# All low parts of the weights on VectorE while the gates of the experts are made

## The chip, the cores and the metric

One core of a Trainium2 chip runs the kernel. The metric is the device time of one execution in microseconds (us). The kernel before was run three times: the median is 3381.05 us, the runs lie between 3377.15 and 3381.17 us. All arithmetic is float32 in effect: TensorE is fed each operand as a high and a low part.

## The reference

The reference is a small network on 256 tokens of width 1024. Ahead of everything else stands a block of two layers, each an attention-like mixer followed by a product-key expert layer (`peer`). After it comes a second block of two layers (feed-forward, four kinds of attention, feed-forward). The change touches the two expert layers alone. Cut to what matters:

```
def peer(x, w_q, subkeys, u_tab, v_tab):
    q = (xf @ w_q).reshape(N, PEER_HEADS, 2, PEER_QHALF)
    s = jnp.einsum('nhpd,hpkd->nhpk', q, subkeys)
    ...
    idx = jnp.take_along_axis(cand_i, best_pos, axis=-1)
    g = jax.nn.softmax(best_s, axis=-1)
    ...
    act = jax.nn.gelu(jnp.einsum('nd,nhkd->nhk', xt, u_tab[it]), approximate=False)
    return jnp.einsum('nhk,nhkd->nd', gt * act, v_tab[it])
```

Each token picks 8 x 16 of 16384 experts. The kernel computes the products with all 16384 rows of `u_tab`, and multiplies the result by a gate matrix that is zero for the experts which a token did not pick; then it multiplies by all of `v_tab`.

## The kernel before, in words

**Weights.** All weights come as 933 units of 128 x 1024 values (512 KB each), which SyncE loads into a ring of four slots (`RAW`, line 2566). A unit is two halves of 128 x 512; the kernel has 1866 halves, numbered `j`. For each half ScalarE copies the raw weight to a rounded high part `WH` (line 1031, `Scalar.split`), and then VectorE or GpSimd subtracts it from the raw weight, which gives the low part `WL` (line 1587, `Vector.split`, or line 2321, `Gpsimd.split`). Here "a low" is one such subtraction. TensorE waits for the low part (line 422, `Tensor.half`) and multiplies three times: high by high, high by low, low by high (line 404). `WH` and `WL` are rings of five halves, so that ScalarE makes the high part of half `j` only when TensorE is through with half `j - 5` (line 1030). A slot of `RAW` is loaded again when the low parts of both of its halves are there (lines 2564 and 2565).

**Who makes a low.** The function `low_on_pool` (line 32) decides it from `j` alone. Its answer is used in four places: in `Vector.split`, in `Gpsimd.split`, and in `Chip.lo`, by which TensorE and SyncE choose the semaphore they wait for. As a rule every fourth half goes to GpSimd (`j % 4 == 3`); in a stretch of 256 halves in each expert layer, every second one does (line 37).

**The expert layer.** `peer_stage` of each engine writes out the order of work: 32 halves for the queries, 256 halves of `u_tab` (groups 0 to 127 of 128 experts), 256 halves of `v_tab`. The gates of groups 0 to 63 (part 0) are made beside the products with groups 64 to 127 of `u_tab`; the gates of groups 64 to 127 (part 1) are made beside the products with groups 0 to 63 of `v_tab`. The stretch of line 37 is just these 256 halves: it begins five halves later than TensorE's count, since the splits run five halves ahead.

**A step of the gates.** A part has 64 steps, one per four tokens, and each engine's `gates` generator is advanced at a rate of 0.55 steps per half (`Pace.tick`). In step s VectorE makes two one-hot tiles, OHA (line 2081, 4 x 128 columns) and OHB (line 2087, 4 x 64 columns). OHB weighted with three parts of the gate gives OHW: ScalarE makes the first part with four instructions (line 1370), GpSimd the second (line 2450), VectorE the third (line 2094). TensorE then runs 12 matmuls of 64 columns (lines 836 to 839), two steps behind, and in every second step VectorE multiplies G, the activations in SBUF, with the result in PSUM (line 2104). OHB of step s waits for all three products of step s - 2 (lines 2084 to 2086); TensorE waits for the same three (lines 832 to 834). GpSimd's product of step s waits for OHB of step s and for the gate matmuls of step s - 2 (lines 2445 to 2447). In VectorE's program a tick's step stands ahead of the tick's low: OHA, OHB, OHW, G in every second step, then lows until the next step. In part 1 there is also GL, the low part of a group of activations (line 2112), once for every two halves.

All two-input operations of VectorE named here read both inputs from SBUF, except G, which reads one from PSUM. Both operations of GpSimd read SBUF.

Of the kernel before, what the change touches and what calls it, by code (L numbers as in the profile page):

```python
# [31 lines left out]
def low_on_pool(j):  # L32

    for layer in range(DEPTH):
        up = BASE[PEER[layer]] + 32 + 2 * GP + NHALF
        if up <= j < up + 4 * (128 - GP):
            return j % 2 == 1
    for end in BASE[1:]:
        if end + 1 <= j <= end + 4:
            return False  # L40
    return j % 4 == 3
# [82 lines left out]
class Chip:  # L124
# [68 lines left out]
    def lo(self, j):  # L193
        return (self.lo_p if low_on_pool(j) else self.lo_v).at(j)
# [1378 lines left out]
class Vector:  # L1573
# [6 lines left out]
    def split(self):  # L1580

        c, e, j = self.c, self.e, self.made
        self.made += 1
        if j < N_HALVES and not low_on_pool(j):
            raw, wh, wl = c.low(j)
            e.wait_ge(*c.hi.at(j))
            e.tensor_tensor(wl, raw, wh.bitcast(F32), ALU.subtract).then_inc(*c.lo_v.mark(j))  # L1587
# [719 lines left out]
class Gpsimd:  # L2307
# [6 lines left out]
    def split(self):  # L2314

        c, e, j = self.c, self.e, self.made
        self.made += 1
        if j < N_HALVES and low_on_pool(j):
            raw, wh, wl = c.low(j)
            e.wait_ge(*c.hi.at(j))  # L2320
            e.tensor_tensor(wl, raw, wh.bitcast(F32), ALU.subtract).then_inc(*c.lo_p.mark(j))  # L2321
# [444 lines left out]
```

## Time and profile before

| | |
|---|---|
| median of 3 runs | 3381.05 us |
| the profiled execution, its own time | 3373.28 us |
| its span in the trace | 3371.3 us |
| TensorE (PE) matmuls busy | 3067.7 us, 91% |
| VectorE (DVE) busy | 2358.2 us, 70% |
| ScalarE (ACT) busy | 1828.7 us, 54% |
| GpSimd (POOL) busy | 1147.1 us, 34% |
| lows on VectorE | 1281, 992.5 us |
| lows on GpSimd | 585, 870.5 us |
| mean granted TensorE clock | 0.975 of full speed |

All times in rows are us from the start of the span unless marked ns. An instruction's duration in the trace runs from its start to its end; instructions of one engine can overlap by a little, so the distance from start to start is what an engine spends on one. A row such as "A <- B: x, n" says that engine and operation A sat idle x us in n cases until B released it. The share of busy time is an average over stages with different limits.

### The profile page before, as it was taken

What the parts mean: (1) busy time and instruction counts of PE and PEld (TensorE: products, weight loads), DVE (VectorE), ACT (ScalarE), POOL (GpSimd) and SP (SyncE); (2) the same over time, 40 slices, a digit from 0 to 9 for tenths busy, and PEclk for the clock granted to TensorE, in tenths of its full rate; (3) what the DMA queues carried; (4) which work ended last, traced back from release to release, by engine and by line L of the source; (5) the groups of instructions that cost most, each with busy time, mean ns of one, the idle gap of its engine ahead of it and who ended that gap; (6) DMA issues with size and microseconds to landing.
All of it is one profiled execution on the core that took longest, in us unless ns stands there. A gap on an engine that the chain in (4) does not pass through costs nothing.

```text
span 3371.3 us, 58728 instructions
## 1 busy us (share of the span) xinstructions
PE 3067.7 (91%) x21820; PEld 2730.0 (81%) x21820; DVE 2358.2 (70%) x4217; ACT 1828.7 (54%) x4063; POOL 1147.1 (34%) x883
## 2 busy tenths in 40 slices
PE   8899988888899889998888889979997999998899
PEld 7699988866688779998886668869876998977798
DVE  4559999899945555999989994564566545456644
ACT  5455566666555445556666555545544555554454
POOL 1113366666522111335666652222110223211121
PEclk9999999999999999999999999989999999999999
DMA  5345543433455325554343335545522555542254
GB/s 208 107 169 169 176 138 132 145 126 125 132 197 196 129 88 169 170 175 138 132 145 126 126 125 202 196 166 191 167 98 82 185 188 193 184 161 82 100 188 157
DMA packets 139532, 512.77 MB, mean 152 GB/s; under 512 B 15713, under 2 KB 16242, under 8 KB 137970
## 3 DMA queue, kind: packets, MB, share of 16 engines
q1 hardware_dynamic: 134352, 489.22, 43.4%
q10 hardware_dynamic: 4898, 19.81, 1.6%
q8 instruction: 175, 2.87, 0.3%
q14 instruction: 107, 0.88, 0.1%
HBM read 507.92 MB, written 1.05 MB: 151 GB/s over the span
## 4 chain that ended last, share of the span: by engine, by line
PE 59%; DVE 25%; issue 8%; POOL 3%; ACT 3%; DMA 1%; DVEq 0%; ACTq 0%; POOLq 0%; SPq 0%
PE ps L404 58%; DVE GAIN L2081 5%; DVE WL L1587 4%; DVE GAIN L2087 4%; DVE OHW L2094 2%; POOL WL L2321 2%; DVE GL L2112 2%; POOL OHW L2450 1%; ACT WH L1031 1%; PE ps L408 1%; ACT BIG L1127 1%; DVE BIG L1699 0%; DVE BIG L1748 0%; DMA RAW<-in_w 0%; DVE XTl L1626 0%
## 5 line engine op out<-in xcount | busy, mean ns | idle before, releaser
L1031 ACT ACTIVATE WH<-RAW 128x512 fp32r<-128x512 f32 x1866 | 1165.4, 628 | 1037.4 <-PE ps L404 1010.8
L2321 POOL TENSOR_TENSOR WL<-RAW,WH 128x512 fp32r<-128x512 f32 x585 | 870.5, 1488 | 2096.6 <-ACT WH L1031 2096.6
L1587 DVE TENSOR_TENSOR WL<-RAW,WH 128x512 fp32r<-128x512 f32 x1281 | 992.5, 779 | 777.7 <-ACT WH L1031 770.7
L404 PE MATMUL ps<-XTh,WH 128*128 128x256 f32 x3928 | 1139.4, 290 | 22.1 <-DVE XTl L1795 8.3
L404 PE MATMUL ps<-XTl,WH 128*128 128x256 f32 x3928 | 1123.1, 286 | 0.0
L404 PE MATMUL ps<-XTh,WL 128*128 128x256 f32 x3928 | 1122.1, 286 | 0.0
L404 PEld LDWEIGHTS ps<-XTh,WH 128*128 128x128 f32 x3928 | 765.5, 195 | 33.4 <-DVE WL L1587 14.1
L404 PEld LDWEIGHTS ps<-XTl,WH 128*128 128x128 f32 x3928 | 766.2, 195 | 3.1
L404 PEld LDWEIGHTS ps<-XTh,WL 128*128 128x128 f32 x3928 | 765.3, 195 | 0.0
L404 PE MATMUL ps<-WH,GH 128*128 128x512 f32 x1408 | 569.9, 405 | 70.4 <-DVE GL L2112 59.6
L404 PE MATMUL ps<-WL,GH 128*128 128x512 f32 x1408 | 553.4, 393 | 0.0
L404 PE MATMUL ps<-WH,GL 128*128 128x512 f32 x1408 | 552.0, 392 | 0.0
L404 PEld LDWEIGHTS ps<-WH,GH 128*128 128x128 f32 x1408 | 266.6, 189 | 137.1 <-DVE GL L2112 68.8
L1370 ACT ACTIVATE OHW<-GAIN,GT 128x64 bf16<-128x64 bf16 x1024 | 270.4, 335 | 107.3 <-DVE GAIN L2087 104.4
L404 PEld LDWEIGHTS ps<-WH,GL 128*128 128x128 f32 x1408 | 266.5, 189 | 57.7
L404 PEld LDWEIGHTS ps<-WL,GH 128*128 128x128 f32 x1408 | 267.2, 190 | 46.7
L2450 POOL TENSOR_TENSOR OHW<-GAIN,GT 128x256 bf16<-128x256 bf16 x256 | 232.2, 908 | 79.9 <-DVE GAIN L2087 79.9
L2081 DVE TENSOR_TENSOR GAIN<-CST,AB 128x512 bf16<-128x512 f32 x256 | 233.0, 910 | 0.0
L404 PEld LDWEIGHTS ps<-OHW,GAIN 128*128 128x128 bf16 x3072 | 106.0, 98 | 143.3 <-issue 125.0
L404 PE MATMUL ps<-OHW,GAIN 128*128 128x64 bf16 x3072 | 133.5, 194 | 89.2 <-DVE OHW L2094 66.8
L2087 DVE TENSOR_TENSOR GAIN<-CST,AB 128x256 bf16<-128x256 f32 x256 | 204.0, 797 | 9.7 <-issue 5.1
L404 PE MATMUL ps<-BIG 128*128 128x64 f32 (+6 forms) x966 | 153.6, 311 | 21.0 <-DVE BIG L1774 4.5
(181 smaller groups left out, 2679.9 us busy)
## 6 DMA issues: line engine op xcount, KB each, us to landing
RAW<-in_w SPq DMA_DIRECT2D x933, 512.0 KB, 3.3
BIG<-in_ln ACTq DMA_DIRECT2D x4, 1024.0 KB, 5.1
GAIN<-in_norms ACTq DMA_DIRECT2D x6, 512.0 KB, 4.2
BIG<-in_sk ACTq DMA_DIRECT2D x2, 1024.0 KB, 4.8
BIG<-in_na_bias ACTq DMA_DIRECT2D x2, 1024.0 KB, 10.5
BIG<-in_qk_gain ACTq DMA_DIRECT2D x2, 960.0 KB, 7.2
BIG<-in_memT ACTq DMA_DIRECT2D x4, 256.0 KB, 7.6
BIG<-in_xT ACTq DMA_DIRECT2D x1, 1024.0 KB, 5.1
```

The lines of the kernel that those rows point to most:

```text
L404: return self.e.matmul(out, lhsT, rhs, start=start, stop=stop, skip_group_check=loose)
L408: return self.e.transpose(out, in_, self.c.IDENT[0:n, 0:n])
L1031: e.activation(wh, raw, ACT.Copy).then_inc(*c.hi.mark(j))
L1127: e.activation(t.E[:, i % 3, w], src[:, w], ACT.Exp, bias=s[:, blk:blk + 1], accum_out=s[:, 2 + blk:3 + blk]).then_inc(*c.exps.mark(tag, i ...
L1370: t = e.activation(c.OHW[:, r, 0, k * GP:k * GP + GP], c.OHB[:, r, k, :], ACT.Copy, scale=c.GT0[:, 4 * s + k:4 * s + k + 1])
L1587: e.tensor_tensor(wl, raw, wh.bitcast(F32), ALU.subtract).then_inc(*c.lo_v.mark(j))
L2081: e.tensor_tensor(c.OHA[:, step % 3], ia, c.AB[:, 0, n4].unsqueeze(2).to_broadcast([P, 4, 128]), ALU.is_equal).then_inc(*c.vec.mark())
L2087: e.tensor_tensor(c.OHB[:, step % 2], ib, c.AB[:, 1, n4].unsqueeze(2).to_broadcast([P, 4, GP]), ALU.is_equal).then_inc(*c.one.mark(stage, ...
L2094: e.tensor_tensor(c.OHW[:, s % 2, 2, :].rearrange("p (k n) -> p k n", k=4), c.OHB[:, s % 2], c.GT[:, 2, 4 * s:4 * s + 4].unsqueeze(2).to_b ...
L2112: e.tensor_tensor(c.GL[:, r, :], c.peer.G[:, g, :], c.GH[:, r, :].bitcast(F32), ALU.subtract).then_inc(*c.xtl.mark(stage, "g", g))
L2321: e.tensor_tensor(wl, raw, wh.bitcast(F32), ALU.subtract).then_inc(*c.lo_p.mark(j))
L2450: e.tensor_tensor(c.OHW[:, r, 1, :].rearrange("p (k n) -> p k n", k=4), c.OHB[:, r], c.GT[:, 1, 4 * s:4 * s + 4].unsqueeze(2).to_broadcast ...
```

## The change

It replaces one line in `low_on_pool`. In the stretch of 256 halves in each expert layer the function now answers False, where it said True for every odd `j`. So 128 lows in each of the two layers move from GpSimd to VectorE, which makes 1537 instead of 1281; GpSimd keeps 329 of 585. Nothing else is changed: neither the order of the work, nor the rate of the gates, nor who makes the three products OHW.

```
--- before.py
+++ after.py
@@ -34,7 +34,7 @@
     for layer in range(DEPTH):
         up = BASE[PEER[layer]] + 32 + 2 * GP + NHALF
         if up <= j < up + 4 * (128 - GP):
-            return j % 2 == 1
+            return False
     for end in BASE[1:]:
         if end + 1 <= j <= end + 4:
             return False
```

## Rows read from the trace of the kernel before

**Rows 1.** The page, part 1: busy time of each engine, share, instructions
```profile
PE 3067.7 (91%) x21820; PEld 2730.0 (81%) x21820; DVE 2358.2 (70%) x4217; ACT 1828.7 (54%) x4063; POOL 1147.1 (34%) x883
```
**Rows 2.** Stretches of the four gate parts: engines' busy us, clock, DMA share, GB/s
```profile
core 0: us, PE busy (x) PEld busy (x) DVE busy (x) ACT busy (x) POOL busy (x), PEclk, DMA share, GB/s
425.50:650.60 225.10, 198.38 (x2123) 191.54 (x2122) 221.07 (x278) 143.47 (x395) 151.34 (x121) 0.99 0.41 136
...
671.70:911.90 240.20, 196.76 (x1440) 148.42 (x1441) 235.66 (x335) 146.48 (x424) 155.97 (x121) 0.99 0.38 127
...
1520.40:1746.10 225.70, 201.81 (x2129) 195.04 (x2128) 218.65 (x278) 143.74 (x396) 150.96 (x121) 0.98 0.40 134
...
1767.20:2009.60 242.40, 199.38 (x1440) 150.56 (x1441) 237.50 (x335) 146.57 (x424) 155.46 (x121) 0.98 0.37 126
```
**Rows 3.** Who waited for whom in 425.5 to 650.6, TensorE and GpSimd
```profile
PE ps L404 <- DVE OHW L2094: 24.8, 23, 2.2
...
POOL OHW L2450 <- DVE GAIN L2087: 20.7, 27, 2.3
```
**Rows 4.** Groups of VectorE in 425.5 to 650.6: count, busy, mean ns, idle before
```profile
L2081 DVE TENSOR_TENSOR GAIN<-CST,AB 128x512 bf16<-128x512 f32 x64 | 66.2, 1035 | 0.0
L1587 DVE TENSOR_TENSOR WL<-RAW,WH 128x512 fp32r<-128x512 f32 x58 | 58.8, 1014 | 1.9 <-ACT WH L1031 1.9
L2087 DVE TENSOR_TENSOR GAIN<-CST,AB 128x256 bf16<-128x256 f32 x64 | 49.1, 768 | 2.9 <-ACT OHW L1370 2.9
L2104 DVE TENSOR_TENSOR BIG<-BIG,ps 128x512 f32<-128x512 f32 x30 | 39.5, 1317 | 0.0
L2094 DVE TENSOR_TENSOR OHW<-GAIN,GT 128x256 bf16<-128x256 bf16 x62 | 30.9, 499 | 0.0
```
**Rows 5.** VectorE in order of time, 496 to 506: start, duration, line
```profile
496.29 1.78 DVE L2081 TENSOR_TENSOR GAIN<-CST,AB 128x512 bf16<-128x512 f32 x1
...
498.32 0.41 DVE L2094 TENSOR_TENSOR OHW<-GAIN,GT 128x256 bf16<-128x256 bf16 x1
498.66 1.09 DVE L1587 TENSOR_TENSOR WL<-RAW,WH 128x512 fp32r<-128x512 f32 x1
...
502.03 1.30 DVE L2104 TENSOR_TENSOR BIG<-BIG,ps 128x512 f32<-128x512 f32 x1
503.25 0.67 DVE L2081 TENSOR_TENSOR GAIN<-CST,AB 128x512 bf16<-128x512 f32 x1
503.85 0.41 DVE L2087 TENSOR_TENSOR GAIN<-CST,AB 128x256 bf16<-128x256 f32 x1
504.18 0.41 DVE L2094 TENSOR_TENSOR OHW<-GAIN,GT 128x256 bf16<-128x256 bf16 x1
504.52 0.67 DVE L1587 TENSOR_TENSOR WL<-RAW,WH 128x512 fp32r<-128x512 f32 x1
505.12 0.67 DVE L2081 TENSOR_TENSOR GAIN<-CST,AB 128x512 bf16<-128x512 f32 x1
```
**Rows 6.** GpSimd in order of time, 496 to 509
```profile
496.08 1.44 POOL L2321 TENSOR_TENSOR WL<-RAW,WH 128x512 fp32r<-128x512 f32 x1 [1.06 <-ACT WH L1031]
498.48 0.73 POOL L2450 TENSOR_TENSOR OHW<-GAIN,GT 128x256 bf16<-128x256 bf16 x1 [0.96 <-DVE GAIN L2087]
...
501.85 0.73 POOL L2450 TENSOR_TENSOR OHW<-GAIN,GT 128x256 bf16<-128x256 bf16 x1 [0.36 <-DVE GAIN L2087]
...
507.58 1.82 POOL L2450 TENSOR_TENSOR OHW<-GAIN,GT 128x256 bf16<-128x256 bf16 x1
```
**Rows 7.** Groups of VectorE in 671.7 to 911.9: lows, GL and OHB
```profile
L2087 DVE TENSOR_TENSOR GAIN<-CST,AB 128x256 bf16<-128x256 f32 x64 | 52.4, 819 | 2.3 <-issue 2.3
...
L1587 DVE TENSOR_TENSOR WL<-RAW,WH 128x512 fp32r<-128x512 f32 x57 | 50.4, 884 | 2.2 <-ACT WH L1031 2.2
...
L2112 DVE TENSOR_TENSOR GL<-BIG,GH 128x256 fp32r<-128x256 f32 x58 | 38.9, 670 | 0.0
```
**Rows 8.** GpSimd in order of time, 700 to 712
```profile
701.13 5.46 POOL L2321 TENSOR_TENSOR WL<-RAW,WH 128x512 fp32r<-128x512 f32 x1 [0.89 <-ACT WH L1031]
```
**Rows 9.** Groups of GpSimd in 425.5 to 650.6
```profile
L2321 POOL TENSOR_TENSOR WL<-RAW,WH 128x512 fp32r<-128x512 f32 x58 | 96.8, 1669 | 56.7 <-ACT WH L1031 56.7
L2450 POOL TENSOR_TENSOR OHW<-GAIN,GT 128x256 bf16<-128x256 bf16 x63 | 57.5, 913 | 20.7 <-DVE GAIN L2087 20.7
```

More of the change, by code:

```diff
@@ L36, in low_on_pool @@
         if up <= j < up + 4 * (128 - GP):
-            return j % 2 == 1
+            return False
     for end in BASE[1:]:
```

## The prediction

> **What bounds the kernel now.** I read the totals first: TensorE is busy for 91% of the span, VectorE for 70% [rows 1]. By this page alone the change looks free: both engines that it touches have room. The totals average over stages, so I cut the span where the change acts, from the first to the last start of OHA (line 2081) in each of the four gate parts [rows 2]. There the picture turns. In part 0 of the first layer VectorE is busy 221.07 of 225.10 us, TensorE 198.38; in part 1 VectorE 235.66 of 240.20, TensorE 196.76. The second layer repeats it (225.70 and 242.40 us long). Inside the gates VectorE is the bound, and the waits agree: TensorE sat 24.8 us until VectorE's OHW [rows 3]. So a change that gives saturated VectorE more work seems wrong, unless its busy time is not all work.
>
> That is what the groups ask [rows 4]. OHA takes 1035 ns on average, a low 1014, OHB 768. In order of time the same operations come out at 0.67 us (OHA, low) and 0.41 us (OHB, OHW) where GpSimd is quiet [rows 5]. Beside GpSimd's low of 1.44 us from 496.08, an OHA takes 1.78 us, 1.11 more [rows 5, 6]. Beside GpSimd's product OHW of 0.73 us from 498.48, a low takes 1.09, 0.42 more. Beside the product from 501.85 the operation that follows is G, and it takes 1.30 us, about its mean of 1317 ns [rows 4, 5]. I read this as: an operation of VectorE with two inputs in SBUF stands still until a GpSimd instruction that got in first is through; G, with one input in PSUM, does not. "Busy" holds these stalls.
>
> **How much of a part is work.** Distances from start to start, undisturbed [rows 5]: OHA 0.60 us (503.25 to 503.85), OHB 0.33, OHW 0.34, low 0.60 (504.52 to 505.12), G 1.22 (502.03 to 503.25). With the counts of [rows 4], part 0 is 64 x 0.60 + 64 x 0.33 + 62 x 0.34 + 58 x 0.60 + 30 x 1.22 = 38.4 + 21.1 + 21.1 + 34.8 + 36.6 = 152.0 us. Idle time is 1.9 + 2.9 = 4.8. The rest of 225.1, **68.3 us**, is stalls. Part 1 has 57 lows and 58 GL; its 335 instructions [rows 2] less these leave the same 220 others. GL has the 256 columns of OHW, so I take 0.34 us: 38.4 + 21.1 + 21.1 + 34.2 + 36.6 + 19.7 = 171.1 us of work, 2.3 + 2.2 = 4.5 idle [rows 7], and **64.6 us** of stalls.
>
> **What is added.** GpSimd's 58 lows of part 0 [rows 9] go to VectorE at 0.60 us, undisturbed: 34.8 us; I take the same 58 for part 1, which has as many instructions of GpSimd [rows 2]. The halves between and behind the parts lie where VectorE has room (TensorE sets the pace there) and are costed at nothing; a part of 128 halves has 116 inside my stretch (58 + 58 lows, [rows 4, 9]), which leaves 6 moved lows outside it; a low is 0.67 us, and TensorE's 198.38 us over 116 halves are 1.7 us for each. Should that cover go, the 12 lows of a layer cost 8 us. The loads from SyncE wait for lows that now come from one engine in order, not later than GpSimd's of 1669 ns [rows 9]; DMA is at 0.41 [rows 2]: nothing.
>
> **What goes.** All stalls behind GpSimd's lows. Those behind its 64 products per part stay. A product starts 0.16 us into VectorE's OHW, once OHB is done [rows 5, 6], and the instruction after OHW decides. In every second step that is G, which does not stall. In the other 32 it is a low, or OHA: 32 x 0.42 = 13.4 us. The two sides of this unknown are 0 (the product never gets in ahead of VectorE) and 64 x 0.42 = 26.9 (each stops one operation). I take the middle, since the row with a low behind OHW and the row with G behind it show just these two cases. With GpSimd free of lows its product no longer comes late, so nobody new waits for it.
>
> **Waits.** VectorE now waits for the high part of twice as many lows: twice 1.9 and 2.2 us, so 3.8 and 4.4. The 2.9 us before OHB were a wait for products, GpSimd's late ones by the program's order; it goes. The bounds here are 0 and what TensorE dictates, below. Queued behind such a wait is the next step's OHA, and behind that all three products; the lows run five halves ahead, which is the cushion.
>
> **The sum.** Part 0: 152.0 + 34.8 + 13.4 + 3.8 = 204.0 us, against 225.1 and 225.7: -21.1 and -21.7. Part 1: 171.1 + 34.8 + 13.4 + 4.4 = 223.7 us, against 240.2 and 242.4: -16.5 and -18.7. Together -78.0 us. TensorE needs 198.38 and 201.81 us in part 0 [rows 2], so it allows this, narrowly; 196.76 and 199.38 in part 1 leave more. The profiled execution took 3373.3 us, so 3295.3 for such a one; the median of the runs lies 7.8 us above it, which gives **3303 us**. Nothing outside the two expert layers changes.
>
> What speaks against the change is advice that the Trainium skill gives in Perfetto Trace Analysis, Optimizing Scalar/DVE Operations: with DVE saturated, moving some of its work to Scalar or even GPSIMD can pay, though the port that DVE and GPSIMD share may make such a move useless. Read by its first half, the change undoes a good offload; by its second half, the offload was worth little. Rows 4 to 6 side with the second half, by 1.11 us of stall for each 0.60 us of saved work where the two collide.
>
> **Rivals.**
>
> *The stalls stay, and it is slower.* The place is VectorE in all four parts; the price is a product of GpSimd that stops two operations instead of half a one. Late products do occur, as the one of 1.82 us from 507.58 [rows 6]. Then 64 x 2 x 0.42 = 53.8 us of stalls remain: part 0 is 152.0 + 34.8 + 53.8 + 3.8 = 244.4, part 1 264.1; +19.3, +18.7, +23.9, +21.7 make +83.6 and 3465 us. It decides from 34.5 us of remaining stalls in part 0 (225.1 - 186.8 - 3.8) and 29.9 in part 1, which is about 0.5 us per product; I forecast 0.21. Against it: products that found GpSimd idle (27 of 63, [rows 3]) show one stall or none in the rows that I have.
>
> If all of today's stalls stayed, which is the offload advice of the skill's page taken plainly, the added 34.8 us in each of four parts would give 3381 + 139 = 3520 us.
>
> *TensorE and VectorE get in each other's way.* In part 0 both then need about 200 us, and each waits for the other's product within two steps (G waits for the gate matmuls, the matmuls for OHW). If 10 us of each part 0 are lost so, 3323 us. For it: both busy times are close. Against it: a step of slack in either direction.
>
> *GpSimd never gets in first.* Its low of 5.46 us [rows 8] shows that it can be held off while VectorE's two-input operations follow each other without a gap. If its product waits until G runs, it ends in time for OHB two steps later, and no stall is left. Part 0 then falls to TensorE's 198.4 and 201.8 (-5.6, -2.2), part 1 by 13.4 twice: 34.6 us less, 3268 us.
>
> *The change does less than it says*: the one function decides for all four users, so I give this no more than a place in "no change", together with an unseen wait that eats just the gain.
>
> **Chances.** Forecast 0.67, TensorE and VectorE in each other's way 0.14, GpSimd never first 0.09, stalls stay 0.07, no change 0.03. About 0.2% (7 us) is what a measurement here can tell from nothing. Faster is 0.90, same 0.03, slower 0.07. The range: 26.9 instead of 13.4 us of stalls adds 54 us, to 3357; no stalls gives 3268. I leave out the outer fifth on either side and take 3275 to 3345, which also holds the second rival.
>
> **What the changed profile would show.** Line 2321 has 329 instructions, and none between the first and last OHA of a part; line 1587 has 1537. The parts last about 204 and 224 us. OHA and OHB fall to near 0.70 and 0.42 us on average, since only GpSimd's products are left and they hit what follows OHW. Of the lows about a quarter take 1.09 us. TensorE's waits for OHW shrink from 24.8 us to a few. Wrong would be: mean OHA or OHB still above 0.9 and 0.6 us (the stalls had another cause); GpSimd's product well above 0.73 us on average (held off); VectorE idle for more than 10 us in part 0 (TensorE, or ScalarE's high parts, became the bound); parts longer than before.

## The result and the profile after

The changed kernel takes 3248.8 us (median of 4 runs, 3243.8 to 3252.1) against 3379.1 us (4 runs) of the kernel before: a ratio of 0.9613, 95% interval 0.9597 to 0.9630. It is 130 us faster. The forecast was faster, 3303 us in a range of 3275 to 3345; the measured time lies below the range.

The same stretches as in [rows 2] for the changed kernel: each gate part from the start of its first OHA to the end of its last (in [rows 2] too a stretch ends with the last OHA's end, not with its start) (columns: length; busy us of TensorE, its weight loads, VectorE, ScalarE, GpSimd; granted clock; DMA share; GB/s):

```profile
428.40:622.30 193.90, 192.93 (x2119) 189.35 (x2118) 193.20 (x335) 141.29 (x395) 88.30 (x63) 1.00 0.48 156
643.70:851.30 207.60, 193.01 (x1441) 147.56 (x1442) 206.27 (x392) 145.17 (x424) 120.10 (x63) 1.00 0.44 144
1457.80:1651.70 193.90, 193.03 (x2119) 189.41 (x2118) 192.96 (x335) 141.30 (x395) 88.30 (x63) 1.00 0.48 156
1673.00:1881.80 208.80, 194.66 (x1441) 148.67 (x1442) 206.19 (x392) 145.31 (x424) 120.09 (x63) 0.99 0.44 143
```

The four parts are shorter by 31.2, 32.6, 31.8 and 33.6 us, 129.2 us together. That is the whole gain: the span of the profiled execution fell by 121.3 us, so the rest of the kernel took 8 us more in this execution. 6.5 of these 8 us lie behind the gates of layer 2, which took 1368.2 us for 1361.7 at a granted clock of 0.960 for 0.969. The moved lows do not explain them: in the twelve traces at the rate of 0.55 this stretch lasts from 1360 us (clock 0.969) to 1373 us (0.959), whoever makes the lows. VectorE executes 57 more instructions in each part (335 for 278, 392 for 335) and is busy for 26 to 31 us less. Now the groups of VectorE in part 0 of layer 1 (beside [rows 4]):

```profile
L1587 DVE TENSOR_TENSOR WL<-RAW,WH 128x512 fp32r<-128x512 f32 x115 | 80.2, 723 | 1.5 <-ACT WH L1031 1.0
L2081 DVE TENSOR_TENSOR GAIN<-CST,AB 128x512 bf16<-128x512 f32 x64 | 43.9, 686 | 0.0
L2087 DVE TENSOR_TENSOR GAIN<-CST,AB 128x256 bf16<-128x256 f32 x64 | 26.4, 412 | 0.0
```

and the same groups and GL in part 1 (beside [rows 7]):

```profile
L1587 DVE TENSOR_TENSOR WL<-RAW,WH 128x512 fp32r<-128x512 f32 x114 | 76.1, 682 | 1.3 <-ACT WH L1031 1.3
L2081 DVE TENSOR_TENSOR GAIN<-CST,AB 128x512 bf16<-128x512 f32 x64 | 43.3, 676 | 0.0
L2087 DVE TENSOR_TENSOR GAIN<-CST,AB 128x256 bf16<-128x256 f32 x64 | 26.2, 410 | 0.0
L2112 DVE TENSOR_TENSOR GL<-BIG,GH 128x256 fp32r<-128x256 f32 x58 | 23.7, 409 | 0.0
```

In part 0 OHA went from 1035 to 686 ns, OHB from 768 to 412. These are about the durations that single undisturbed instructions had before [rows 5]. The lows in part 1, at 682 ns, show next to no stall; in part 0, at 723 ns, they show a little. That is better than was forecast: a quarter of them were to be stopped by GpSimd's products. The products themselves tell what happened. First part 0, then part 1:

```profile
L2450 POOL TENSOR_TENSOR OHW<-GAIN,GT 128x256 bf16<-128x256 bf16 x63 | 88.3, 1411 | 108.1 <-DVE GAIN L2087 108.1
L2450 POOL TENSOR_TENSOR OHW<-GAIN,GT 128x256 bf16<-128x256 bf16 x63 | 121.2, 1941 | 107.8 <-DVE GAIN L2087 107.8
```

GpSimd, free of its lows, takes longer for a product than before (1411 and 1941 ns against 913, [rows 9]). Now it is GpSimd's product that stands still while VectorE goes on. VectorE in order of time in part 1 shows one case:

```profile
658.10 0.41 DVE L2094 TENSOR_TENSOR OHW<-GAIN,GT 128x256 bf16<-128x256 bf16 x1
658.43 0.67 DVE L1587 TENSOR_TENSOR WL<-RAW,WH 128x512 fp32r<-128x512 f32 x1
659.03 0.41 DVE L2112 TENSOR_TENSOR GL<-BIG,GH 128x256 fp32r<-128x256 f32 x1
...
660.91 0.41 DVE L2094 TENSOR_TENSOR OHW<-GAIN,GT 128x256 bf16<-128x256 bf16 x1
661.24 1.28 DVE L2104 TENSOR_TENSOR BIG<-BIG,ps 128x512 f32<-128x512 f32 x1
```

and GpSimd beside it:

```profile
658.24 3.55 POOL L2450 TENSOR_TENSOR OHW<-GAIN,GT 128x256 bf16<-128x256 bf16 x1 [3.34 <-DVE GAIN L2087]
```

The product starts 0.14 us into OHW and ends at 661.79. Six more instructions of VectorE with two SBUF inputs follow at their undisturbed durations (the fence leaves out three); only with G, at 661.24, does the product get through, 0.55 us later.

### The profile page after: what moved, and what is told of

Same layout as the page of the kernel before. It is cut to its first block, busy times and chain, and to the rows that moved or that the text cites. A ratio compares the mean times of both kernels' runs of the same rounds, so it can differ in the third digit from the quotient of the medians.

```text
span 3250.0 us, 58728 instructions
## 1 busy us (share of the span) xinstructions
PE 3053.4 (94%) x21820; PEld 2725.8 (84%) x21820; DVE 2256.2 (69%) x4473; ACT 1820.9 (56%) x4063; POOL 913.7 (28%) x627
## 4 chain that ended last, share of the span: by engine, by line
PE 65%; DVE 26%; issue 4%; ACT 3%; POOL 1%; DMA 1%; DVEq 0%; ACTq 0%; SPq 0%
PE ps L404 64%; DVE WL L1587 7%; DVE GAIN L2081 4%; DVE BIG L2104 2%; DVE GAIN L2087 2%; DVE OHW L2094 2%; ACT WH L1031 1%; PE ps L408 1%; POOL OHW L2450 1%; DVE GL L2112 1%; DMA RAW<-in_w 1%; ACT BIG L1127 1%; DVE BIG L1748 0%; DVE BIG L1699 0%; DVE XTl L1626 0%
## 5 line engine op out<-in xcount | busy, mean ns | idle before, releaser
L1587 DVE TENSOR_TENSOR WL<-RAW,WH 128x512 fp32r<-128x512 f32 x1537 | 1108.8, 731 | 765.2 <-ACT WH L1031 757.5
L2321 POOL TENSOR_TENSOR WL<-RAW,WH 128x512 fp32r<-128x512 f32 x329 | 440.4, 1339 | 1852.5 <-ACT WH L1031 1852.5
L2450 POOL TENSOR_TENSOR OHW<-GAIN,GT 128x256 bf16<-128x256 bf16 x256 | 421.6, 1661 | 436.0 <-DVE GAIN L2087 436.0
L2081 DVE TENSOR_TENSOR GAIN<-CST,AB 128x512 bf16<-128x512 f32 x256 | 174.8, 683 | 0.0
L2104 DVE TENSOR_TENSOR BIG<-BIG,ps 128x512 f32<-128x512 f32 x128 | 170.5, 1332 | 1.3 <-PE ps L404 1.3
L404 PEld LDWEIGHTS ps<-BIG 128*128 128x128 f32 (+4 forms) x966 | 124.1, 190 | 48.5 <-issue 22.5
L404 PE MATMUL ps<-WH,XTh 128*128 128x512 f32 (+1 forms) x400 | 158.2, 395 | 3.4 <-DVE XTl L1626 1.3
```

The source lines that it names most:

```text
L404: return self.e.matmul(out, lhsT, rhs, start=start, stop=stop, skip_group_check=loose)
L2081: e.tensor_tensor(c.OHA[:, step % 3], ia, c.AB[:, 0, n4].unsqueeze(2).to_broadcast([P, 4, 128]), ALU.is_equal).then_inc(*c.vec.mark())
L2104: e.tensor_tensor(g, g, c.B[4 + (s // 2) % 2][:, :].rearrange("p (n i) -> p n i", n=8), ALU.mult).then_inc(*c.gated.mark(stage, part, s))
L2450: e.tensor_tensor(c.OHW[:, r, 1, :].rearrange("p (k n) -> p k n", k=4), c.OHB[:, r], c.GT[:, 1, 4 * s:4 * s + 4].unsqueeze(2).to_broadcast ...
```

## The experiments

The theory after the result: GpSimd's reads of SBUF stopped VectorE for 65 to 68 us per part, and the change gave this back. The rivals: GpSimd's slow results were waited for; any instruction of GpSimd has the effect; the parts depend on each other. What remained to be explained besides was why the products cost almost nothing now.

**Part 0 alone and part 1 alone.** Edit of the changed kernel, the other half of the stretch as before:

```
-        if up <= j < up + 4 * (128 - GP):
+        if up <= j < up + 2 * (128 - GP):
             return False
+        if up <= j < up + 4 * (128 - GP):
+            return j % 2 == 1
```

(and the mirror image for part 1).

> The change in the first 128 halves of each stretch alone (part 0); part 1 as before. If each part gains by itself: parts 0 last 194 us, parts 1 240 to 242 us, the kernel 3379 - 63 = 3316 us. If the gain of one part hangs on the other (a lag that is carried over): parts 1 shorten too, below 235 us, and the kernel is under 3305 us.

> The change in the last 128 halves of each stretch alone (part 1). Each by itself: parts 0 stay at 225 us, parts 1 last 207 to 209 us, the kernel 3379 - 66 = 3313 us. Carried over: another sum than that of the two runs (130 us together).

Measured: 3313.7 us (2 runs) and 3306.2 us (2 runs), against 3375.8 us of the kernel before beside them: 62.1 and 69.6 us, 131.7 together, where both changes at once give 130. With part 0 changed, it lasts 193.9 us and part 1 still 242.0; with part 1 changed, part 0 lasts 223.4 and part 1 208.8. Each part gains by itself, and nothing to speak of is carried over (before: 225.1 and 240.2 us).

**GpSimd writes, but does not read.** The kernel before, with one line for GpSimd's lows in the stretches:

```
-            e.tensor_tensor(wl, raw, wh.bitcast(F32), ALU.subtract).then_inc(*c.lo_p.mark(j))
+            e.memset(wl.bitcast(F32), 0.0).then_inc(*c.lo_p.mark(j))
```

> The kernel before, in which GpSimd in the stretches fills the low part with zeros (it reads nothing) in place of subtracting: the low parts of every second half are left out there. VectorE has the work of before. Theory (GpSimd's reads of SBUF stop VectorE): OHA falls to 0.68 us and OHB to 0.41 on average, VectorE's work is 152 and 171 us, and TensorE sets both parts: about 194 and 191 us, the kernel about 3379 - 160 = 3219 us. Rival (any instruction of GpSimd stops VectorE, or its writes do): OHA stays near 0.9 to 1.0 us, the parts over 210 us.

Measured: 3204.7 us (2 runs), 171 us below the kernel before. Part 0 and part 1 of layer 1:

```profile
425.80:617.50 191.70, 191.70 (x2116) 189.03 (x2116) 164.12 (x278) 141.28 (x395) 73.77 (x120) 1.00 0.47 159
639.20:829.10 189.90, 187.49 (x1439) 146.84 (x1440) 180.71 (x335) 144.35 (x424) 97.02 (x121) 1.00 0.47 159
```

OHA among VectorE's groups in part 0:

```profile
L2081 DVE TENSOR_TENSOR GAIN<-CST,AB 128x512 bf16<-128x512 f32 x64 | 43.7, 683 | 0.0
```

and the fills among GpSimd's:

```profile
L2322 POOL MEMSET WL<- 128x512 f32 x57 | 30.0, 526 | 118.8 <-ACT WH L1031 118.8
```

VectorE has the work of before and GpSimd as many instructions, yet OHA is at 683 ns for 1035. The fills are shorter than the subtractions were, but 30.0 us of them in part 0 leave no stall on OHA. So GpSimd's writes do not stop VectorE; that its reads do, the next run shows. SBUF — State Buffer of the Trainium skill (Who interferes with whom) says the same of VectorE instructions with two SBUF inputs: they contend with a GpSimd instruction that reads SBUF and not with one that only writes it. This run and the next agree. The fills also give TensorE's own pace, since TensorE is busy all of 191.70 us in part 0: 191.7 and 189.9 us. (The low parts are zeros there; the run below that keeps them, with products that read nothing, has TensorE busy for all of 192.10 us.) The changed kernel is 2.2 us above that in part 0 and 17.7 us in part 1, where the added lows do have their price.

**Reads that nobody waits for.** The changed kernel, in `Gpsimd.split`, layer 2 alone:

```
+        if j % 2 == 1 and 0 <= j - BASE[PEER[1]] - 165 < 256:
+            e.wait_ge(*c.hi.at(j))
+            k = c.CST[:, 0:256].unsqueeze(1).to_broadcast([P, 2, 256])
+            e.wait_ge(*c.pool.now())
+            e.tensor_tensor(c.KM[:, :, :], k, k, ALU.subtract).then_inc(*c.pool.mark())
```

> The changed kernel, in which GpSimd in layer 2's stretch alone also subtracts constants from constants at the 128 old places, same size (128x512), a result that nobody waits for. VectorE makes all lows. Theory: all the stalls of before come back on top of the added work: part 0 of layer 2 187 + 68 = about 255 us, part 1 206 + 65 = about 271 us, the kernel 3249 + 61 + 62 = 3372 us. Rival (before, the time went to waits for GpSimd's slow lows, not to stalls of VectorE): nobody waits here, so at most a few late products: under 3270 us. Layer 1 stays as in the changed kernel in both.

Measured: 3341.7 us (2 runs), 93 us above the changed kernel. The two parts of layer 2:

```profile
1457.70:1696.20 238.50, 201.21 (x2124) 193.31 (x2124) 238.21 (x335) 143.90 (x395) 144.03 (x119) 0.99 0.38 127
1717.50:1977.70 260.20, 202.82 (x1443) 150.37 (x1444) 258.05 (x392) 147.91 (x426) 168.16 (x121) 0.99 0.34 116
```

They are longer by 44.6 and 51.4 us, for 58 reads each whose result is used nowhere: 0.8 to 0.9 us for one. VectorE is busy for 238.21 of 238.50 us, so the added time is in its instructions' durations and not in waits, for late products neither. The waits for GpSimd's slow lows are thereby out as the cause. The size is three quarters of what was expected (61 and 62 us); what makes the difference to the 1.1 to 1.2 us per low of before was not found.

**Every fourth low.** In the stretches `return j % 4 == 3`, so that GpSimd keeps 64 lows per layer.

> In the stretches GpSimd keeps every fourth low (j % 4 == 3), 64 per layer in place of 128 or none. Stalls in proportion to GpSimd's lows: part 0 about 152 + 17 + 34 + 4 = 207 us, part 1 about 171 + 17 + 32 + 4 = 224 us, the kernel 3379 - 65 = 3314 us, halfway. If stalls only come where two lows of GpSimd follow closely: near the changed kernel, under 3270 us. If a few of GpSimd's lows are hidden beside G and pay off in part 1: part 1 under 205 us.

Measured: 3326.0 us (4 runs), ratio 0.9859 (0.9838 to 0.9880). Part 0 lasts 205.7 us, as expected, part 1 231.4 us, 7 longer than expected. With 29 lows on GpSimd, VectorE's work in part 1 is 171.1 + 17.4 = 188.5 us, and 42.9 us are stalls and waits, those by products among them: 1.5 us per low of GpSimd, for 0.60 us of work saved. A quarter of the lows on GpSimd does not pay here either.

**The products without their reads.** The changed kernel, `e.memset(c.OHW[:, r, 1, :], 0.0)` in the place of GpSimd's product.

> The changed kernel, in which GpSimd fills its product OHW with zeros (it reads nothing): the second part of each gate is left out. It shows what the 256 products still cost. Theory (a held-off product costs VectorE nothing; only the few that get in ahead of a low do): part 0 falls from 194 to about 191 us, where the run with zeroed low parts found TensorE's floor, part 1 stays within 2 us of 207.7, the kernel about 3249 - 8 = 3241 us. Rival (the products still cost what the prediction had, 13.4 us per part): part 1 falls to about 195 us, the kernel to about 3218 us.

Measured: 3243.9 us (4 runs, 3237.6 to 3246.5), 5 us less than the changed kernel, with runs that overlap its own. The two parts of layer 1:

```profile
429.00:621.10 192.10, 192.10 (x2116) 189.04 (x2115) 188.09 (x335) 141.29 (x395) 19.61 (x63) 1.00 0.46 158
642.80:849.80 207.00, 194.07 (x1441) 147.44 (x1442) 205.52 (x392) 145.21 (x424) 19.60 (x63) 1.00 0.42 145
```

Part 0 is shorter by 1.8 us, part 1 by 0.6. In part 0 TensorE hides the rest, so VectorE's busy time is the better measure: 188.09 for 193.20 us, and 205.52 for 206.27. The products' reads cost VectorE 5.1 us in part 0 and 0.8 us in part 1. The forecast had 13.4 us in each.

**No lows on GpSimd at all.** `low_on_pool` answers False everywhere; 329 more lows move.

> No lows on GpSimd anywhere: the other 329 go to VectorE too. Outside the gates VectorE has room in most stretches, but not where the experts are searched (300 to 428 us: 117 of 127.5 us busy, [rows of after]). Theory (each low of GpSimd costs VectorE more in stalls than the 0.60 us it saves): faster by 5 to 20 us, 3229 to 3244 us. Rival (where VectorE is not saturated the stalls cost nothing, and in the search the added lows count): same or slower by up to 12 us, 3249 to 3261 us.

Measured: 3248.9 us (4 runs), the changed kernel's time. The theory as stated fell: a low of GpSimd costs nothing on the whole where TensorE sets the pace. In the search of the experts VectorE is busier than in the changed kernel (122.85 of 127.8 us, for 116.97 of 127.5) and the search ends no sooner.

**Another rate.** `pace.rate = 0.52` for `0.55` in `peer_stage` of all four engines, in the changed kernel.

> The changed kernel with the gates at 0.52 steps per half in place of 0.55, so that the 66 steps of a part fill all 128 halves. Part 1 is VectorE's (207.7 us against TensorE's floor of 189): some 7 halves less stand behind the gates at TensorE's pace, so part 1 is longer by itself but ends the layer 3 to 5 us sooner; part 0 is at TensorE's floor and does not change. The kernel 3249 - 8 = 3241 us. Rival (the last steps collide with the end of the part, where G and the next groups wait for the last gate): 5 to 10 us slower, 3257 us.

Measured: 3234.1 us (4 runs, 3233.1 to 3235.5), ratio 0.9582 (0.9566 to 0.9598): 15 us below the changed kernel, and with the late product at the same rate the best version that computes everything. Part 0 runs at TensorE's pace, busy for 202.23 of 202.40 us. From the start of layer 1's gates to that of layer 2's it saves 3.5 us in the profiled executions (1025.9 for 1029.4), which is the expected size. In layer 2 the gates end 3.1 us later (427.1 for 424.0 us from their start), and what follows is some 9 us shorter where traces of like clock are compared (1352.1 us at 0.968 against 1361.7 of the kernel before at 0.969; 1359.4 against 1368.2 of the changed kernel, both at 0.960, with the late product below). By this estimate layer 2 gains about 6 us and both together 9 to 10; the remaining 5 us of the 15 stay open.

**A late product.** The changed kernel, with GpSimd's product also waiting for VectorE's OHW of the step before:

```
+                if s:
+                    e.wait_ge(*c.ohw_v.at(stage, part, s - 1))
```

> The changed kernel, in which GpSimd's product of step s also waits for VectorE's OHW of the same step of its program (step s - 1), so that it begins about 0.4 us later, when VectorE is already in the instruction behind OHW. Theory (a product is held off when a two-input instruction of VectorE is under way and the next stands ready behind it): in no case does it stop the low behind OHW; lows average 0.69 us, part 0 falls from 193.2 to about 191 us, part 1 stays; about 3249 - 6 = 3243 us. Rival (who gets in first is settled afresh at each instruction's end): a product now stops the second operation behind OHW as often as before the first; part 0 stays at 193 us or above, OHA or lows over 0.72 us; 3249 us or more.

> The late product and the rate of 0.52 together, as a version that may beat both kernels. The rate alone gave 3234 us. If the two gains add up: about 3228 us. If at this rate part 0 is no longer at its limit: 3234 us.

> The changed kernel once more, as the measure for the two versions beside it: 3249 us, 0.961 to 0.963 of the kernel before.

Measured, 5 runs each beside one another: changed kernel 3249.0 us, late product 3248.2 us, late product with rate 0.52 3234.8 us. Part 0 stays at 193.9 us. That the product stops nothing when it begins later did not come true: where two lows follow OHW, it often stops the second. VectorE's two lows then take 1.70 us (1.27 undisturbed) beside the product of 0.91 us:

```profile
481.41 1.70 DVE L1587 TENSOR_TENSOR WL<-RAW,WH 128x512 fp32r<-128x512 f32 x2
```

```profile
481.65 0.91 POOL L2452 TENSOR_TENSOR OHW<-GAIN,GT 128x256 bf16<-128x256 bf16 x1 [2.87 <-DVE OHW L2094]
```

The second low by itself, and the high part that it waits for:

```profile
482.10 1.01 DVE L1587 TENSOR_TENSOR WL<-RAW,WH 128x512 fp32r<-128x512 f32 x1
```

```profile
481.44 0.63 ACT L1031 ACTIVATE WH<-RAW 128x512 fp32r<-128x512 f32 x1 [0.73 <-PE ps L404]
```

It begins 0.69 us after the first in place of 0.60, since ScalarE's high part ends at 482.07. The product got in during this gap of 0.09 us.

**A gap in VectorE's row.** What decides, then, whether a product gets in first? I took from the traces each product that starts within 0.22 us of the start of an OHW which is not followed by G, and counted how many instructions of VectorE had followed each other up to that OHW without a gap or a stop. "Stops" means that the instruction behind OHW is lengthened by about 0.42 us:

| kernel | products | with 4 or fewer unbroken ahead of OHW | with 5 or more |
|---|---|---|---|
| before | 46 | 45 of 46 stop the next | no such case |
| changed | 128 | 7 of 8 | 0 of 120 |
| every fourth low | 67 | 59 of 59 | 0 of 8 |

The late products start one instruction on, in a low. 121 of them do so with 5 or more unbroken instructions ahead. Where the next instruction follows without a gap, none of 93 is stopped; where a gap of 0.04 to 0.24 us stands just ahead of it, 27 of 27 are (behind the one longer gap, of 0.40 us, the product was through). With the rate of 0.52 it is 0 of 72 and, up to 0.26 us, 46 of 46. So the late product did not refute that a sequence without a gap holds products off: its stops lie where VectorE itself waited. The test makes a gap by hand, in VectorE's `gates` ahead of OHA:

```
+                if step and step % 2 == 0:
+                    e.wait_ge(*c.lo_v.now())
+                    e.wait_ge(*c.xtl.now())
```

> The changed kernel, in which VectorE before OHA of every even step waits for its own instruction before (a wait that costs it some 0.15 to 0.2 us and nobody else anything). Theory, formed from the counts in the traces (a product of GpSimd gets in ahead of a two-input instruction only if VectorE's row of them has been broken within its last 4 instructions, and is held off until G once 5 or more have followed each other without a gap): each product of the even steps now stops the low behind OHW, 32 x 0.42 = 13.4 us per part, besides 32 x 0.17 = 5 us for the gaps themselves: part 1 lasts 206.9 + 18.5 = about 225 us, its lows average about 0.77 us, GpSimd's product averages 0.73 us in place of 1.94, the kernel is slower by about 2 x 18.5 us for the parts 1 and up to 2 x 15 us for the parts 0, 3285 to 3315 us. Rival (GpSimd's lows themselves, by keeping the port busy, were what let the products in): only the gaps are paid, part 1 lasts 212 us, the product stays above 1.5 us, the kernel 3260 us.

Measured: 3306.5 us (4 runs), ratio 0.9772 (0.9756 to 0.9789), 58 us slower than the changed kernel. The stretches of layer 1:

```profile
425.60:632.20 206.60, 195.89 (x2124) 191.57 (x2123) 202.97 (x335) 141.93 (x395) 46.18 (x63) 0.99 0.45 147
652.90:879.50 226.60, 202.65 (x1443) 149.91 (x1444) 221.55 (x392) 146.56 (x425) 45.86 (x63) 0.98 0.40 132
```

Groups in 660 to 870, first GpSimd's product, then VectorE's low:

```profile
L2453 POOL TENSOR_TENSOR OHW<-GAIN,GT 128x256 bf16<-128x256 bf16 x59 | 43.1, 730 | 169.7 <-DVE GAIN L2090 169.7
```

```profile
L1587 DVE TENSOR_TENSOR WL<-RAW,WH 128x512 fp32r<-128x512 f32 x107 | 83.7, 798 | 0.0
```

VectorE in order of time, and then GpSimd's product beside it:

```profile
745.48 0.68 DVE L1587 TENSOR_TENSOR WL<-RAW,WH 128x512 fp32r<-128x512 f32 x1
746.25 0.69 DVE L2084 TENSOR_TENSOR GAIN<-CST,AB 128x512 bf16<-128x512 f32 x1
746.86 0.42 DVE L2090 TENSOR_TENSOR GAIN<-CST,AB 128x256 bf16<-128x256 f32 x1
747.19 0.42 DVE L2097 TENSOR_TENSOR OHW<-GAIN,GT 128x256 bf16<-128x256 bf16 x1
747.53 1.10 DVE L1587 TENSOR_TENSOR WL<-RAW,WH 128x512 fp32r<-128x512 f32 x1
```

```profile
747.35 0.73 POOL L2453 TENSOR_TENSOR OHW<-GAIN,GT 128x256 bf16<-128x256 bf16 x1 [3.52 <-DVE GAIN L2090]
```

The low at 745.48 is followed by OHA after 0.77 us in place of 0.60, a gap of 0.17. Three instructions on, the product gets in and the low behind OHW takes 1.10 us. It happens so with 127 of 128 products that are followed by a low. Part 1 lasts 226.6 us (225 expected), the product 730 ns on average. No low of GpSimd was needed for it: a gap of 0.17 us alone turns these products from free to 0.42 us each. A gap at another distance from the product was not tried by hand.

## Why the prediction was wrong, and where it was right

**What bounds the kernel**: right. VectorE in all four parts; the whole gain lies in them. After the change TensorE is as much the bound of part 0, with 0.8 us of waits for OHW left of 24.8 [rows 3]; in part 1 VectorE is still the bound, busy for 206.27 of 207.60 us.

**Work and stalls of before**: right. With the added lows the prediction has 186.8 and 205.9 us of work, and where neither GpSimd's lows nor its products read (the products without their reads) VectorE is busy for 188.1 and 205.5 us. OHA, OHB and, in part 1, the low have fallen to the durations that the single rows gave. That the stalls come from GpSimd's reads is shown by the fills and by the idle reads.

**The halves outside the parts, the loads**: costed at nothing, which held. The stretch between the parts lasts 21.4 and 21.3 us (21.1 before), the one between the layers' gates 606.5 us (608.5), and the parts hold all of the gain.

**The remaining stalls**: this is the step that failed. "The row with a low behind OHW and the row with G behind it show just these two cases", and so 32 x 0.42 = 13.4 us were set per part, with 3.8 and 4.4 us of waits. The products' reads cost VectorE 5.1 and 0.8 us instead, and its waits are 1.5 and 1.3 us. Left over beside the work were 193.9 - 186.8 = 7.1 us in part 0 and 207.6 - 205.9 = 1.7 us in part 1, in place of 17.2 and 17.8. The four parts together are 51 us below the forecast sum of 855.4 us, which is nearly all of the miss of 54 us in the median. The prediction's own sign for this came: "GpSimd's product well above 0.73 us on average (held off)". The row itself was read rightly. But all 46 products counted in the kernel before met a VectorE whose sequence had just been broken by a stop, 36 of them by one beside a low of GpSimd, and in that state products get in first. Without the lows the sequence mostly stays whole, and the products are held off. The stalls by products were for the most part a consequence of the stalls by lows. The rival "GpSimd never gets in first" named just this, from the low of 5.46 us [rows 8], and got a chance of 0.09. A row that contradicts the chosen one should have widened the range to its end, 3268 us, though that too lies above the measured time, for the reason that follows.

**TensorE's floor**: too high. I took its busy time in part 0, 198.38 us, as what it needs, and by it capped that rival at 3268 us. The run with fills has 191.7 us and the changed kernel 193.9. Here the busy time of an engine that also waits was more than its need. Without this cap the rival is 3303 - 4 x 13.4 = 3249 us, and 3248.8 us was measured. That it fits so closely is luck: it stands for parts of 190.6 and 210.3 us, and measured were 193.9 and 207.6 us (208.8 in layer 2), whose errors cancel.

**The offload advice** that the Trainium skill gives in Perfetto Trace Analysis, Optimizing Scalar/DVE Operations (with DVE saturated, moving work to GPSIMD can pay, but the shared port may undo it): its second half holds here, at 0.60 us saved and 1.2 us lost per low on average in part 0 (68.3 us of stalls over 58 lows, the products' stalls among them) and 1.1 us in part 1.

## What to carry to other kernels

Work that is moved from a saturated VectorE to GpSimd pays only if what the move stops is less than what it saves; compare the mean duration of each group with that of a single undisturbed instruction before trusting "busy". Costs that two engines inflict on each other need not shrink in proportion: taking the lows away freed VectorE of most of the products' stalls too, and a gap of 0.17 us brought these back. When rows of the trace show both states of such a contest, price both, and ask which of them the change will bring about.

## What the hardware showed that was not expected

A GpSimd instruction that reads SBUF can be kept waiting across many VectorE instructions with two SBUF inputs, not just until the end of the one under way: 3.55 us over seven of them, until G with its PSUM input. The Trainium skill, in SBUF — State Buffer (SBUF: two separate sides), has the pair of ports go to whichever instruction starts first, for the whole of that instruction; the runs agree for one instruction, and add that an unbroken sequence of VectorE keeps the port from one instruction to the next. In the four kernels counted, none of 128 products stopped VectorE with 5 or more unbroken instructions ahead of the OHW in which it started, and 238 of 241 did with 4 or fewer. A gap just ahead of the next instruction lets a product in as well, however long the sequence before it: 73 of 73 for gaps of 0.04 to 0.26 us in the two kernels with the late product, against 0 of 165 without a gap. Why the length of the sequence decides in the first case stays open, as does whether the limit is the same in other mixes of instructions.
